# Two delta rule layers of a four-layer network: keys projected first, vector lengths taken per token, the small projections streamed over tokens, the local projections spread among the levels, and fewer idle products at the RMS norms

## The chip, the cores and the metric

One core of a Trainium2 chip runs the whole program as one launch. The metric is the device time of that launch in microseconds (us). The engines are PE (TensorE, the matrix products), DVE (VectorE), ACT (ScalarE), POOL (GpSimd) and SP (SyncE, which issues the weight loads). Each engine runs its own list of instructions strictly in order, and engines wait for one another on semaphores.

## The reference, cut to what matters

Input is 256 tokens of 1024 features. Layers 0 and 1 (softmax attention, a dense and a routed feed-forward) are not touched. Layers 2 and 3 each do this:

```python
h = rmsnorm(x, pre_mix_norm[l]); proj = h @ w_in[l]
a_qkv, a_z, a_b, a_a, b_q, b_k, b_v = split(proj)   # 3*512, 512, 4, 4, 512, 512, 512
a_qkv = silu(causal_dwconv(a_qkv, dn_conv))         # 4 taps along the tokens
aq, ak, av = l2norm(q), l2norm(k), v                # 4 heads of 128; l2norm: x * rsqrt(sum x*x + eps)
beta = sigmoid(a_b); g = -exp(a_log) * softplus(a_a + dt_bias)
o_a = gated_delta_rule(aq, ak, av, g, beta)         # needs the inverse of a unit lower triangular matrix
o_a = rmsnorm(o_a, out_norm) * silu(a_z)
o_b = dilated_attention(rope(b_q), rope(b_k), b_v)  # 8 heads of 64
x = x + rmsnorm(concat(o_a, o_b) @ w_out[l], post_mix_norm[l])
x = x + rmsnorm(conv_glu_ffn(rmsnorm(x, pre_ffn_norm[l])), post_ffn_norm[l])
```

## The kernel before, in words

Weights stream from HBM in units of 128 x 2048 float32 (1 MB) in the order that `stream_order` lists, into six buffers (`raw`). ACT rounds each unit to `w_hi` (L513) and DVE subtracts to get the rest, `w_lo` (L518). These two steps are the split. There are three buffers for split units, so the unit three places further in the stream can only be split when PE has read the present one. `walk("in", L, i)`, which stands in ACT's list and in DVE's, is that place: "unit i is read, now split the one three further on". Each projection product is done three times (hi*hi, hi*lo, lo*hi) by `mm3` (L758).

The input projection `in` has 14 units. Units 0 to 5 are query, key and value of the delta rule, two units each, done by `features` with the features on the partitions (products over 256 tokens). Numbers 3 to 6 (units 6 to 13) are the gate z, the local queries, the local keys and the local values, done by `part` in four pieces of 12 products over 512 columns (two token tiles t, two halves i of the inner dimension). Two small matrices for beta and decay, `wba`, have 8 columns.

PE's function `delta` of a layer goes in this order before the change: three projected blocks with the queries first; the 8-column products (token tiles as the stationary operand, 8 columns streamed, 48 products); projection 3; four products of ones with the squares (L1077), which give each head's length in every row, 128x512 each; projection 4; running sums of the decay (L1087, `gcol`), the decay and beta spread over rows (L1094, `grow` and `brow`); transposes of keys and values (L1102, `kn`, `vn`); the products key*key and key*query (L1112, `kk`, `kq`). Then come LEVELS = 7 levels, which invert the triangular matrix by blocks. Level 0 is a transpose (L1127); each further level is 8 products X (L1129), a copy by ACT (L1568), then 16 products D and DT (L1146), which DVE subtracts (L2196). One quarter of projection 5 stands between X and D in each of levels 1 to 4. After the levels stand eight groups of state and output products (L1157 to L1185), projection 6, the transposes of the outputs (L1194, `oT`), and then `local_attention`, which turns the rotated queries and keys (L833) and starts its scores (L804).

DVE, meanwhile: three convolution taps per block (L2084); the lengths' reciprocal (L2114) and the scaling of q and k (L2115) over 128x512 elements, four times; the decay matrix `gam` (L2127, masks added; ACT takes its exp, L1562); the blocks for the levels (L2172); after the levels the outputs, the rotation of the local queries and keys (`rope`, L1768 to L1773), and then the split of `aT_lo`, the low part of the transposed outputs (L2239).

Before the delta layer stands `enter`, the RMS norm: DVE makes a diagonal matrix from the rows' norms (`pre_scale`, L1892 and L1893), PE multiplies each token tile by it (L736), DVE applies the norm's weights (`pre_turned`, L1902, weights `prew`), ACT and DVE split the result (L1305, L1749). Between the two token tiles PE does idle products (`keep_warm`, L753), whose result nobody reads: WARM_PRE = 6 of them at the entrance of layer 2, WARM_RMS = 9 at the other three (layer 2 before the feed-forward, layer 3 twice).

## Time and profile before

| what | value |
|---|---|
| median of 3 runs | 2441.65 us (2441.45 to 2452.83) |
| profiled execution, its own time | 2445.3 us |
| its span in the trace | 2443.5 us |
| PE busy | 2290.4 us, 94% |
| DVE busy | 1745.2 us, 71% |
| ACT busy | 1382.3 us, 57% |
| mean granted TensorE clock | 0.966 of full |

PE is the engine that is nearly always busy, so a stretch gets shorter where PE has fewer or cheaper instructions, where PE waits less, or where it runs less long at the lower clock. "Busy" counts a product's whole latency; how much time a row of products takes is read from the distance of their starts.

### The profile page before, as it was taken

The page shows a single profiled execution, that of the slowest core. Times are in us where ns is not written, and L with a number is a line of the kernel's source. Part 1 is how long each engine was busy: PE and PEld are TensorE (multiplying, and loading weights), DVE is VectorE, ACT ScalarE, POOL GpSimd, SP SyncE. Part 2 cuts the span into 40 slices and gives each one's busy share as a digit, 9 for nine tenths or more (in the row PEclk, how much of TensorE's full clock was granted, in tenths as well). Part 3 has the DMA queues.
Part 4 walks back from the last instruction along what each step waited for, and adds up shares of the span by engine and source line. Part 5 has one row for each costly group of instructions (what it writes and reads, how often), then busy time and mean ns, then how long its engine had stood idle before and what let it go on. Part 6 is the DMA issues. An engine that isn't in the chain of part 4 may idle for free. (4 is left out here: it accounts for less than half of the span.)

```text
span 2443.5 us, 32636 instructions
## 1 busy us (share of the span) xinstructions
PE 2290.4 (94%) x12462; PEld 1917.8 (78%) x12462; DVE 1745.2 (71%) x1861; ACT 1382.3 (57%) x1440; POOL 55.0 (2%) x72
## 2 busy tenths in 40 slices
PE   7899999789999999999999999898799989888998
PEld 5599987568787878787878776687679978777997
DVE  5555557568888888888888898567557666765776
ACT  5433334547777777777777766352545445344544
POOL 2000000010000000000000020000000000000000
PEclk9899999899999999999999999889899999899999
DMA  9355555249999999999999998331225543122551
GB/s 390 143 194 183 183 187 173 77 153 381 355 380 359 381 356 380 358 378 359 379 359 380 358 389 324 139 138 44 95 97 183 188 157 121 69 78 96 183 188 52
DMA packets 81800, 573.37 MB, mean 235 GB/s; under 512 B 9552, under 2 KB 9664, under 8 KB 15984
## 3 DMA queue, kind: packets, MB, share of 16 engines
q1 hardware_dynamic: 76320, 545.82, 59.8%
q0 software_dynamic: 5376, 26.11, 2.9%
q8 instruction: 71, 1.16, 0.2%
q14 instruction: 33, 0.27, 0.0%
HBM read 564.03 MB, written 17.83 MB: 238 GB/s over the span
## 5 line engine op out<-in xcount | busy, mean ns | idle before, releaser
L518 DVE TENSOR_TENSOR w_lo<-raw,w_hi 128x2048 fp32r<-128x2048 f32 x508 | 1165.1, 2300 | 385.3 <-ACT w_hi L513 384.1
L513 ACT CAST w_hi<-raw 128x2048 fp32r<-128x2048 f32 x508 | 969.2, 1910 | 538.1 <-PE bank L758 532.0
L758 PE MATMUL bank<-w_hi,xT_hi 128*128 128x512 f32 x1184 | 476.1, 402 | 7.3 <-DVE w_lo L518 5.0
L758 PE MATMUL bank<-w_lo,xT_hi 128*128 128x512 f32 x1184 | 469.7, 397 | 0.0
L758 PE MATMUL bank<-w_hi,xT_lo 128*128 128x512 f32 x1184 | 468.8, 396 | 0.0
L758 PE MATMUL bank<-xT_hi,w_hi 128*128 128x256 f32 x1344 | 380.9, 283 | 11.9 <-DVE xT_lo L1749 10.0
L758 PE MATMUL bank<-xT_lo,w_hi 128*128 128x256 f32 x1344 | 380.2, 283 | 0.0
L758 PE MATMUL bank<-xT_hi,w_lo 128*128 128x256 f32 x1344 | 380.1, 283 | 0.0
L758 PE MATMUL bank<-w_hi,aT_hi 128*128 128x512 f32 x864 | 349.5, 405 | 15.1 <-DVE aT_lo L1954 9.3
L758 PE MATMUL bank<-w_lo,aT_hi 128*128 128x512 f32 x864 | 342.9, 397 | 0.0
L758 PE MATMUL bank<-w_hi,aT_lo 128*128 128x512 f32 x864 | 342.1, 396 | 0.0
L758 PEld LDWEIGHTS bank<-w_hi,xT_hi 128*128 128x128 f32 x1184 | 223.6, 189 | 67.7 <-DVE w_lo L518 9.6
L758 PEld LDWEIGHTS bank<-xT_hi,w_hi 128*128 128x128 f32 x1344 | 255.9, 190 | 14.1 <-DVE xT_lo L1749 10.6
L758 PEld LDWEIGHTS bank<-w_hi,xT_lo 128*128 128x128 f32 x1184 | 223.3, 189 | 54.8
L758 PEld LDWEIGHTS bank<-w_lo,xT_hi 128*128 128x128 f32 x1184 | 223.5, 189 | 53.6 <-issue 1.6
L758 PEld LDWEIGHTS bank<-xT_lo,w_hi 128*128 128x128 f32 x1344 | 256.1, 191 | 1.4
L758 PEld LDWEIGHTS bank<-xT_hi,w_lo 128*128 128x128 f32 x1344 | 256.0, 191 | 0.0
L758 PEld LDWEIGHTS bank<-w_hi,aT_hi 128*128 128x128 f32 x864 | 163.3, 189 | 54.4 <-issue 18.1
L758 PEld LDWEIGHTS bank<-w_hi,aT_lo 128*128 128x128 f32 x864 | 163.0, 189 | 40.0
L758 PEld LDWEIGHTS bank<-w_lo,aT_hi 128*128 128x128 f32 x864 | 163.4, 189 | 34.7
L1435 ACT ACTIVATE arena<-bank,fcw 128x256 f32<-128x256 f32 x88 | 45.0, 562 | 59.0 <-PE bank L758 59.0
L1568 ACT COPY arena<-bank 128x512 f32<-128x512 f32 x24 | 14.1, 587 | 85.7 <-PE bank L1129 85.7
(310 smaller groups left out, 1794.4 us busy)
## 6 DMA issues: line engine op xcount, KB each, us to landing
raw<-in_wu_eg SPq DMA_DIRECT2D x112, 1024.0 KB, 7.2
raw<-in_wu_eu SPq DMA_DIRECT2D x112, 1024.0 KB, 7.1
raw<-in_wu_ed SPq DMA_DIRECT2D x112, 1024.0 KB, 7.1
raw<-in_wu_up SPq DMA_DIRECT2D x44, 1024.0 KB, 4.8
raw<-in_wu_ffn_gu SPq DMA_DIRECT2D x28, 1024.0 KB, 4.8
raw<-in_wu_in SPq DMA_DIRECT2D x28, 1024.0 KB, 4.8
raw<-in_wu_down SPq DMA_DIRECT2D x22, 1024.0 KB, 4.8
raw<-in_wu_ffn_d SPq DMA_DIRECT2D x14, 1024.0 KB, 4.8
```

The lines of the kernel that those rows point to most:

```text
L513: nc.scalar.copy(w_hi[:, place(i), :], src).then_inc(*E.hi.mark("unit", i))
L518: nc.vector.tensor_tensor(w_lo[:, place(i), :], raw[:, i % RAW, :], w_hi[:, place(i), :].bitcast(F32), ALU.subtract) \
L758: mm = nc.tensor.matmul(o, l[i], r[j], start=(first and n == 0), stop=(last and n == 2), skip_group_check=not lone)
L1435: ins = nc.scalar.activation(buf[:, s % 2, m, :], bank[b + half][:, m * S:(m + 1) * S], ACT.Identity, bias=fcw[:, c, 3:4], scale=fcw[:, c, ...
L1568: nc.scalar.copy(dn["Xl"][:, t * DN_H:(t + 1) * DN_H, :], bank[t][:, :].rearrange("p (h n) -> p h n", n=P)) \
```

## The change

- **Order of the projected blocks.** The key block comes first, then query, then value. The stream's order of units is 2, 3, 0, 1, 4, ... to fit. `grow` is done after the query block, `brow` after the value block, each between projected blocks, and the transposes and key products between the halves of projection 3.
- **Lengths per token.** Instead of four products of 128x512 that put a head's length into every row, 8 products with one streamed column each give the length of (token, head) as one number (`lengths`), for keys and for queries. Keys and queries are no longer scaled themselves. The numbers go where a per-token factor stands anyway: into `gam`, `kdsc`, `bexp`, the spread beta (`brk`), and for queries into the last RMS norm (`rq`, `rq2`).
- **Small projections.** `wba` is the stationary operand (16 columns: high and low parts) and the 256 tokens are streamed; 16 products instead of 48; two small products (`fold`) bring the result back to tokens. It stands at the head of `delta`. Sigmoid is now 1/(1+exp(-x)), sharing ACT's exp.
- **Local projections among the levels.** Projections 4 and 5 both lie in levels 2 to 5, one quarter before and one after D of each level.
- **The end.** `rope` goes ahead of the outputs in DVE's list; the local queries and keys are turned before the outputs (`turn_outputs`), in other banks, and the split of `aT_lo` goes behind.
- **Entrance.** WARM_RMS is 4 and the entrance of layer 2 has no idle products. `wba`, `cw` and `prew` of both layers are loaded early (`load_both`). At layer 2, both norms are taken before the first `pre_turned`, and DVE's two splits of units stand behind.

```diff
 UNIT = 2048
-WARM_START, WARM_LN, WARM_PRE, WARM_RMS = 6, 5, 6, 9
...
                 else:
-                    yield from [(("in", L, i), "wu_in", (L - 2, i)) for i in range(14)]
...
+            def load_both():
+                gp.wait_ge(*params.last())
+                for L in (2, 3):
+                    load((wba[:, L - 2, :, :], A["wba"][L - 2], ("wba", L)), (cw[:, L - 2, :, :], A["cw"][L - 2], ("cw", L)),
+                         (prew[:, L - 2, :, :], A["prew"][L - 2], ("prew", L)))
...
-                     (fcw[:, :, :], A["fcw"][L - 2], ("fcw", L)), (prew[:, :, :], A["prew"][L - 2], ("prew", L)),
-                     (onorm[:, :], A["onorm"][L - 2], ("onorm", L)))
+                load((fcw[:, :, :], A["fcw"][L - 2], ("fcw", L)), (onorm[:, :], A["onorm"][L - 2], ("onorm", L)))
             gp.dma_start(cst[:, :], A["cst"]).then_inc(*consts.mark())
...
+                turn_heads(L, "k", lambda t, c: both(t, 4 + c), lambda t: roped.at(L, t, 0), 6)
+                turn_outputs(L)
                 turned_heads(L, 0, 0)
-                turned_heads(L, "k", 2)
...
+                def lengths(name, src, b):
+                    o = open_bank(M, b)
+                    for t in range(NT):
+                        for h in range(DN_H):
+                            c = t * DN_H + h
+                            mm = nc.tensor.matmul(o[:, c:c + 1], src[:, h, t * P:(t + 1) * P], ones[:, 0:1], start=True, stop=True)
+                    mm.then_inc(*M.groups.mark(name, L))
+
+                def project(nb, b0, units=range(2)):
+                    features([bank[b0 + j] for j in range(2)], ("in", L, 2 * nb), ("in", L, 2 * nb + 1),
+                             lambda j, m: (2 * j + m) * P, ("unit", "in", L, 2 * nb),
+                             [("cv", L, 2 * nb), ("cv", L, 2 * nb + 1)], units)
+
+                pe.wait_ge(*wsmall.at("wba"))
+                o = open_bank(M, 6)
+                for kc in range(KC):
+                    nc.tensor.matmul(o[0:16, 0:S], wba_s[:, L - 2, kc, :], xT[0][:, kc, :], start=(kc == 0), stop=False,
+                                     skip_group_check=True)
+                    mm = nc.tensor.matmul(o[0:8, 0:S], wba_s[:, L - 2, kc, 0:8], xT[1][:, kc, :], start=False, stop=(kc == KC - 1),
+                                          skip_group_check=True)
...
-                for g in range(4):
-                    pe.wait_ge(*squares.at(L, g))
-                    o = open_bank(M, 4 + g)
-                    nc.tensor.matmul(o[:, :], ones, dn["sq"][:, 4 * (g % 2):4 * (g % 2) + 4, :].rearrange("p a b -> p (a b)"),
-                                     start=True, stop=True).then_inc(*M.groups.mark("ssq", L, g))
...
+                project(1, 0, (0,))
+                pe.wait_ge(*M.free[6].at("ba", L))
+                o = open_bank(M, 7)
+                for t in range(NT):
+                    mm = nc.tensor.matmul(o[:, t * 8:t * 8 + 8], dn["baT"][:, t * P:(t + 1) * P], C("fold")[0:16, :],
+                                          start=True, stop=True)
+                mm.then_inc(*M.groups.mark("ba8", L))
+                project(1, 0, (1,))
+                for j in range(2):
+                    open_bank(M, 2 + j)
+                project(0, 2)
+                pe.wait_ge(*squares.at(L, "k"))
+                lengths("ssk", dn["sqk"], 6)
 
...
+                pe.wait_ge(*decay.at(L, "gB"))
+                for t in range(NT):
+                    heads(open_bank(M, 4 + t), "grow", t, product(lambda h: dn["gB"][:, t * DN_H + h, :], lambda h: C("upto")))
+                for j in range(2):
+                    open_bank(M, j)
+                project(2, 0)
+                pe.wait_ge(*decay.at(L, "bB"))
+                for t in range(NT):
+                    heads(open_bank(M, 2 + t), "brow", t, product(lambda h: dn["bB"][:, t * DN_H + h, :], lambda h: ident))
+                pe.wait_ge(*squares.at(L, "q"))
+                lengths("ssq", dn["sqq"], 7)
+                for t in range(NT):
+                    part("in", L, "in", 3, xT, 4, 0, t)
+                for t in range(NT):
+                    heads(open_bank(M, t), "kn", t, turn_feature(DN_H, t))
+                for t in range(NT):
+                    pe.wait_ge(*M.free[2 + t].at("brow", L, t))
+                    heads(open_bank(M, 2 + t), "kk", t, product(lambda h: dn["cv"][:, DN_H + h, t * P:(t + 1) * P],
+                                                                lambda h: dn["kb"][:, h, t * P:(t + 1) * P]))
+                for t in range(NT):
+                    part("in", L, "in", 3, xT, 4, 1, t)
+
+                pe.wait_ge(*M.act.at("silu", L, 5))
+                for t in range(NT):
+                    heads(open_bank(M, 6 + t), "vn", t, turn_feature(2 * DN_H, t))
+                for t in range(NT):
+                    heads(open_bank(M, 4 + t), "kq", t, product(lambda h: dn["cv"][:, DN_H + h, t * P:(t + 1) * P],
+                                                                lambda h: dn["cv"][:, h, t * P:(t + 1) * P]))
...
-                    if n <= 4:
-                        part("in", L, "in", 5, xT, 6, (n - 1) // 2, (n - 1) % 2)
+                    filler = {2: (4, 0), 3: (4, 1), 4: (5, 0), 5: (5, 1)}.get(n)
+                    if filler:
+                        part("in", L, "in", filler[0], xT, 6, filler[1], 0)
...
+                    if filler:
+                        part("in", L, "in", filler[0], xT, 6, filler[1], 1)
...
+            def turn_outputs(L):
                 for t in range(NT):
                     pe.wait_ge(*gated.at(L, t))
-                    o = open_bank(M, t)
+                    o = open_bank(M, 2 + t)
                     for h in range(DN_H):
                         mm = nc.tensor.transpose(o[:, h * P:(h + 1) * P], dn["o"][:, t * DN_H + h, :], ident)
                     mm.then_inc(*M.groups.mark("oT", L, t))
...
-                enter("in", WARM_PRE if L == 2 else WARM_RMS)
+                enter("in", 0 if L == 2 else WARM_RMS)
...
-                for g in range(4):
-                    ve.wait_ge(*M.free[4 + g].at("len", L, g))
-                    v = dn["cv"][:, 2 * g:2 * g + 2, :].rearrange("p a b -> p (a b)")
-                    ln = dn["sq"][:, 4 * (g % 2):4 * (g % 2) + 4, :].rearrange("p a b -> p (a b)")
-                    chain(V_.reciprocal(ln, ln))
-                    V_.scalar_tensor_tensor(v, v, (float(P) ** -0.5 if g < 2 else 1.0), ln, ALU.mult, ALU.mult) \
-                        .then_inc(*normed.mark(L, g))
-                ve.wait_ge(*normed.at(L, 3))
...
+                spread(dn["gB"], gl, "gB")
+                conv(3, 1)
+                walk("in", L, 3)
+                walk("in", L, 0)
+                conv(0, 2)
+                conv(1, 3)
+                sync()
+
+                ve.wait_ge(*M.free[6].at("ssk", L))
...
+                token_keys()
+                decayed("kk", 2, dn["AT"])
                 level_blocks(0)
-                token_keys()
-                decayed("kq", 2, dn["qk"])
+                decayed("kq", 4, dn["qk"])
+                walk("in", L, 6)
...
+                    sync()
+                    level_block(1, t)
                 token_values()
+                walk("in", L, 7)
...
-                    if n in (1, 3, 5):
-                        walk("in", L, 9 + (n - 1) // 2)
-
+                    if n >= 3:
+                        walk("in", L, 5 + n)
...
+                rope(L, (("in", 4, 6), ("in", 5, 6)), 0, 16,
+                     C("cos2").rearrange("p (a b) -> p a b", b=8), C("sin2").rearrange("p (a b) -> p a b", b=8))
...
+                ve.wait_ge(*M.act.at("oss", L))
+                V_.tensor_tensor(ss, ss, rq2, ALU.mult).then_inc(*decay.mark(L, "ss"))
                 ve.wait_ge(*M.act.at("ort", L))
                 chain(V_.reciprocal(rn8, rn8))
+                chain(V_.tensor_tensor(rn8, rn8, rq, ALU.mult))
...
-                rope(L, (("in", 4, 0), ("in", 5, 6)), 0, 16,
-                     C("cos2").rearrange("p (a b) -> p a b", b=8), C("sin2").rearrange("p (a b) -> p a b", b=8))
                 walk("in", L, 12)
...
+                if (L, which) == (2, "in"):
+                    pre_scale(L, which, rt, 1)
                 pre_turned(L, which, 0)
-                pre_scale(L, which, rt, 1)
+                if (L, which) != (2, "in"):
+                    pre_scale(L, which, rt, 1)
                 rest_T((L, which), L, 0)
                 pre_turned(L, which, 1)
                 rest_T((L, which), L, 1)
...
                     pre_scale(L, "in", "in", 0)
+                    enter(L, "in", "in")
+                    ve.wait_ge(*M.act.at("wba"))
+                    V_.tensor_tensor(wba_s[:, :, :, 8:16], wba[:, :, :, :], wba_s[:, :, :, 0:8].bitcast(F32), ALU.subtract) \
+                        .then_inc(*wsmall.mark("wba"))
                     walk("pg", 1, 2)
-                    enter(L, "in", "in")
                     walk("pg", 1, 3)
                 delta(L)
-                walk("in", L, 13)
```

Three places in the engines' lists. The first is DVE in `delta`, where lengths and decay are made (`w_lo<-raw,w_hi` is a split; the rows of the changed kernel have its own line numbers). Before:

```order
L518 TENSOR_TENSOR w_lo<-raw,w_hi 128x2048 x2
L2114 RECIPROCAL arena<-arena 128x512
L2115 SCALAR_TENSOR_TENSOR arena<-arena 128x512
...
L2115 SCALAR_TENSOR_TENSOR arena<-arena 128x512
L518 TENSOR_TENSOR w_lo<-raw,w_hi 128x2048
L2126 TENSOR_TENSOR small<-bank,small 128x4
L2127 TENSOR_TENSOR arena<-bank,msk 128x512 x2
L2132 TENSOR_TENSOR arena<-arena,bank 128x4x128 x2
```

After:

```order
L2167 RECIPROCAL small<-small 128x8
L2168 TENSOR_TENSOR small<-small 128x8
L2140 COPY arena<-small 128x1024
L2176 TENSOR_TENSOR small<-bank,small 128x4
L2177 TENSOR_TENSOR arena<-bank,msk 128x512 x2
L525 TENSOR_TENSOR w_lo<-raw,w_hi 128x2048
L2182 TENSOR_TENSOR small<-small 128x4
L2183 TENSOR_TENSOR small<-small 128x4
L2187 TENSOR_TENSOR arena<-arena,small 128x512 x2
L525 TENSOR_TENSOR w_lo<-raw,w_hi 128x2048
```

The four reciprocals over 128x512 and the four scalings (one pair of them shown) are gone; in their place stand operations on 8 numbers a row and one scaling of the decay matrix (L2187).

The second is DVE from the last level to the start of the local attention in layer 3 (`vec` holds the local queries and keys). Before:

```order
L518 TENSOR_TENSOR w_lo<-raw,w_hi 128x2048
L2196 TENSOR_TENSOR arena<-arena,bank 128x512 x2
L2207 COPY arena<-bank 128x512
...
L2219 TENSOR_TENSOR arena<-arena,bank 128x512
L2222 RECIPROCAL small<-small 128x8
L2227 SCALAR_TENSOR_TENSOR arena<-arena,small,onorm 128x128 x8
L2232 TENSOR_TENSOR arena<-arena 128x512 x2
L1768 TENSOR_TENSOR arena<-vec,cst 128x128
...
L518 TENSOR_TENSOR w_lo<-raw,w_hi 128x2048
L2239 TENSOR_TENSOR aT_lo<-bank,aT_hi 128x4x128 x2
L518 TENSOR_TENSOR w_lo<-raw,w_hi 128x2048
```

After:

```order
L2269 TENSOR_TENSOR arena<-arena,bank 128x512 x2
L525 TENSOR_TENSOR w_lo<-raw,w_hi 128x2048
L1815 TENSOR_TENSOR arena<-vec,cst 128x128
L1816 TENSOR_TENSOR arena<-vec,cst 128x128
...
L2281 COPY arena<-bank 128x512
L2284 TENSOR_TENSOR R<-arena,bank 128x512
L2288 TENSOR_SCALAR arena<-bank,small 128x128 x4
L2293 TENSOR_TENSOR arena<-arena,bank 128x512
...
L2309 TENSOR_TENSOR arena<-arena 128x512 x2
L525 TENSOR_TENSOR w_lo<-raw,w_hi 128x2048 x2
L1893 TENSOR_TENSOR aT_lo<-bank,aT_hi 128x4x128 x2
```

The rotation moved from behind the outputs to ahead of them, one more split stands ahead of it, and the subtraction for `aT_lo` stands behind both last splits.

The third is PE at the entrance of layer 2 (`R` is the diagonal matrix, `cst` the idle products). Before:

```order
L736 MATMUL bank<-R,X 128x128 x8
L753 MATMUL bank<-cst 128x512 x6
L736 MATMUL bank<-R,X 128x128 x8
L758 MATMUL bank<-xT_hi,w_hi 128x256
L758 MATMUL bank<-xT_lo,w_hi 128x256
```

After:

```order
L748 MATMUL bank<-R,X 128x128 x16
L1096 MATMUL bank<-xT_hi,wba_hi_lo 16x256
L1098 MATMUL bank<-xT_lo,wba_hi_lo 8x256
L1096 MATMUL bank<-xT_hi,wba_hi_lo 16x256
L1098 MATMUL bank<-xT_lo,wba_hi_lo 8x256
```

The idle products between the two tiles are gone, and the small projection stands first, with 256 columns streamed by each of its products.

## Rows read from the trace of the kernel before

**Rows 1.** The page, part 1: busy us (share) xinstructions.
```profile
PE 2290.4 (94%) x12462; PEld 1917.8 (78%) x12462; DVE 1745.2 (71%) x1861; ACT 1382.3 (57%) x1440; POOL 55.0 (2%) x72
```

**Rows 2.** Layer 3, PE's timeline: start, us, engine, line, operation.
```profile
2021.55 0.36 PE L758 MATMUL bank<-xT_hi,w_hi 128*128 128x256 f32 x1 [2.49 <-DVE xT_lo L1749]
...
2109.50 0.71 PE L1127 MATMUL bank<-cst,arena 128*128 128x128 f32 x5
...
2160.17 0.35 PE L1157 MATMUL bank<-R,arena 128*128 128x128 f32 x1 [0.83 <-DVE arena L2196]
...
2178.78 0.60 PE L1194 MATMUL bank<-cst,arena 128*128 128x128 f32 x4
...
2190.11 0.80 PE L804 MATMUL bank<-arena 64*128 64x128 f32 x4 [0.98 <-ACT arena L1318]
```

**Rows 3.** The same five places in layer 2.
```profile
1579.14 0.36 PE L758 MATMUL bank<-xT_hi,w_hi 128*128 128x256 f32 x1 [2.49 <-DVE xT_lo L1749]
...
1670.32 0.50 PE L1127 MATMUL bank<-cst,arena 128*128 128x128 f32 x3
...
1722.54 0.46 PE L1157 MATMUL bank<-R,arena 128*128 128x128 f32 x2 [0.83 <-DVE arena L2196]
...
1741.15 0.49 PE L1194 MATMUL bank<-cst,arena 128*128 128x128 f32 x3
...
1752.48 0.80 PE L804 MATMUL bank<-arena 64*128 64x128 f32 x4 [0.98 <-ACT arena L1318]
```

**Rows 4.** PE's waits from 1975 to 2235: us in total, times, longest.
```profile
PE bank L833 <- DVE aT_lo L2239: 5.7, 1, 5.7
PE bank L1129 <- DVE arena L2172: 5.5, 1, 5.5
```

**Rows 5.** Layer 3, PE's timeline: small projection, a filler, one level.
```profile
2055.71 0.17 PE L758 MATMUL bank<-wba_hi,xT_hi 128*128 128x8 f32 x1
...
2061.00 0.78 PE L758 MATMUL bank<-w_hi,xT_hi 128*128 128x512 f32 x1
...
2143.71 0.48 PE L758 MATMUL bank<-w_hi,xT_hi 128*128 128x512 f32 x1
...
2146.58 3.73 PE L1146 MATMUL bank<-arena 128*128 128x128 f32 x32
2150.15 1.95 PE L1129 MATMUL bank<-arena 128*128 128x128 f32 x16
```

**Rows 6.** Layer 3, DVE's timeline: taps, reciprocal, split, transposed keys.
```profile
2031.71 5.28 DVE L2084 SCALAR_TENSOR_TENSOR arena<-bank,cw,arena 128x255 f32<-128x255 f32 x12
...
2095.88 3.35 DVE L2114 RECIPROCAL arena<-arena 128x512 f32<-128x512 f32 x1
...
2099.99 2.29 DVE L518 TENSOR_TENSOR w_lo<-raw,w_hi 128x2048 fp32r<-128x2048 f32 x1
...
2109.20 2.16 DVE L2153 TENSOR_SCALAR R<-bank,small 128x128 f32<-128x128 f32 x8
```

**Rows 7.** Entrance of layer 3: timelines of PE, DVE and ACT.
```profile
2009.25 7.89 PE L753 MATMUL bank<-cst 128*128 128x512 f32 x18
...
2015.27 1.29 DVE L1902 TENSOR_TENSOR arena<-bank,prew 128x512 f32<-128x512 f32 x2 [4.60 <-DMA onorm<-in_onorm]
...
2012.15 1.88 ACT L513 CAST w_hi<-raw 128x2048 fp32r<-128x2048 f32 x1
```

**Rows 8.** Before layer 3's feed-forward: timelines of PE and DVE.
```profile
2234.78 7.89 PE L753 MATMUL bank<-cst 128*128 128x512 f32 x18
...
2239.18 0.29 DVE L1893 TENSOR_SCALAR R<-cst,small 128x128 f32<-128x128 f32 x1
```

**Rows 9.** Entrance of layer 2: PE's timeline.
```profile
1569.55 5.32 PE L753 MATMUL bank<-cst 128*128 128x512 f32 x12
```

**Rows 10.** PE's timeline, and its window: busy PE, PEld, DVE, ACT, POOL, PEclk, DMA.
```profile
1995.22 0.47 PE L758 MATMUL bank<-w_hi,aT_hi 128*128 128x512 f32 x1 [4.32 <-DVE aT_lo L1954]
...
1996.00:1999.50 3.50, 3.50 (x10) 2.73 (x9) 0.00 (x0) 0.69 (x2) 0.00 (x0) 0.52 0.43 178
```

333 lines of the change are left out of this document (166 added, 167 removed).

## The prediction

> **What bounds the kernel now.** I read the page first: PE is busy 94% of the span [rows 1], so only what PE does or waits for counts. Then I read PE's timeline over the changed stretch, from the first projected block to the first score product of the local attention. It takes 168.6 us in layer 3 [rows 2] and 173.3 us in layer 2 [rows 3], and four places cut it in pieces:
>
> - A, first block to level 0: 88.0 us in layer 3, 91.2 in layer 2.
> - B, the levels: 50.7 and 52.2.
> - C, states, outputs and projection 6: 18.6 and 18.6.
> - D, end of projection 6 to the first score: 11.3 and 11.3.
>
> PE's list of waits shows what interrupts it: 5.7 us before the turned queries for `aT_lo`, 5.5 us in level 1 for DVE's blocks [rows 4], and small ones of 1 to 3 us around the lengths and transposes. The same stand in layer 2. Last I read the granted clock: after a wait of 4.3 us TensorE is at the lower of its two levels, 1.2 instead of 2.4 GHz (0.52 of full), for the 3.5 us shown [rows 10]; PE is busy there and loses half, 1.7 us. Such stretches recur behind the waits of both layers.
>
> **Prices on PE, from distances of starts.** From 2021.55 to 2055.71 PE does six units of 48 products over 256 tokens: 0.119 us a product, 5.7 a unit [rows 2, 5]. The 48 small products take 5.3 us [rows 5]. A quarter of a projection (12 products of 512 columns) takes 2.9 us, 2143.71 to 2146.58, and 16 products of 128x128 take 3.6 us, 2146.58 to 2150.15, so four heads cost 0.9 [rows 5].
>
> **Piece A after.** The small projection is 16 products over 256 tokens, 1.9 us, and two fold products, which no row shows; bounds 0.1 and 0.5, I take 0.3. Six units: 34.3. Lengths: 16 float32 products in two groups, with one streamed column and a 128x128 stationary operand, which no row shows. The products of 128x128 are 0.22 each, which gives 3.6, and the 8-column ones 0.11 each, which gives 1.8 [rows 5]; I take the upper, being float32 too, and 0.1 a group for its end: 3.8. The running sum is 0.5. Six pairs of four-head groups (`grow`, `brow`, `kn`, `kk`, `vn`, `kq`) are 10.8. Projection 3 is 11.3. Sum 62.9 us. Projection 4, 11.3 us, has left for the levels.
>
> Does PE wait in it? I laid the three lists side by side with the durations of [rows 6]: three tap pairs of two halves 5.3 us, a split 2.3 on DVE and 1.9 on ACT. ACT's squares of the keys are ready at 21 us and PE asks for them at 25. The spread beta comes at 31, asked for at 41. The unit for projection 3 is split at 35, asked for at 45; the first block of level 0 is ready at 56, asked for at 63. The least slack is 4 us, and the four reciprocals of 3.35 us with their scalings, which stood ahead of the transposes [rows 6], are gone. So I cost the new DVE and ACT work in A at nothing; PE's own 62.9 us hide it. Were that cover gone, the price would be what each lateness adds, at most the 16 us the reciprocals and scalings had. A falls by 88.0 - 62.9 - 11.3 = 13.8 us in layer 3 and 17.1 in layer 2, net of the moved projection.
>
> **Piece B after.** PE's own: 43.7 us as before (level 0 1.8, six times X 1.8, five times D 3.6, the last D 1.8, four quarters 11.3) and 11.3 for projection 4. Levels 2 to 5 are then bound by PE, 11 us each, and DVE's 2.8 us of subtractions hide. Levels 0 and 1 stay bound by DVE: a split of 2.3 us stands right where level 0's transpose comes out, then the two halves (0.7 three times each), then the values' scaling (2.2, as the keys' in [rows 6]) and another split ahead of level 2's blocks. I get waits of 3.4 + 1.1 before level 1 and 2.5 + 0.5 before level 2. ACT empties projection 4's banks in level 4 only behind its two copies: 1.5 us. The last subtraction: 1.0. So waits are 9.9 against 7.0 before (50.7 - 43.7). B loses 2.9 us in layer 3, 1.3 in layer 2.
>
> **Piece C after.** DVE has a split and the rotation (3 us) ahead of the first output copy now, so the last output product waits some 1.5 us. C loses 1.3.
>
> **Piece D after.** The rotation is done long before. Turned queries and keys (3.6 us) and outputs (1.8) follow projection 6 at once; ACT splits one unit, then copies (2.4 us), and is done with the keys when PE is. First score 5.4 us after projection 6, not 11.3: a gain of 5.9 in each. DVE's subtraction for `aT_lo` comes just as the first scores are ready and delays them by under 0.3.
>
> So the pieces give 15.5 us in layer 3 and 20.4 in layer 2, with PE at full clock and no wait but those named. From that I take two stretches of lower clock a layer (after level 0's wait, and after the one-column products or the last output), 3.4 us, and 1.5 us a layer for small waits that I don't see: 10.6 + 15.5 = 26.1 us.
>
> **The entrances.** Layer 3 before: DVE waits 4.6 us for weights queued with `prew` [rows 7]; early loading removes it, and with four idle products (3.5 us at 7.9 for nine) the second tile starts at about 2012.8, not 2017.0. Next late is ACT, whose split of 1.9 us lies ahead of its copies until 2014.0 [rows 7]. The first block starts at about 2018.7 instead of 2021.55: 2.85 us less, but PE then stands still 4 us instead of 2.5, for which I charge one lower-clock stretch: 1.2 net. Before each feed-forward the second diagonal is ready at 2239.5 and the idle products end at 2242.6 [rows 8]: 3.0 us to gain with four idle products, less 0.8 for clock, twice: 4.4. Entrance of layer 2: six idle products stood some 5.1 us between the tiles [rows 9]. They go, and DVE's and ACT's chain behind the first tile, no longer covered, gives back 1.0: 4.1. Together 9.7.
>
> POOL issues three more small loads ahead of the experts' collection, at 0.5 us each; no engine waits for them. Two fewer activation table loads a layer lie on ACT, which has slack in A.
>
> **A rule against it.** In the trace a gap of 4.3 us was followed by half clock [rows 10]; the gap of 2.5 us at 2021.55 [rows 2] was followed by six units at 0.119 us a product throughout. So by the rows I charge 1.7 us for the entrance of layer 3 and 0.8 for each of the two before a feed-forward, 3.3 in all. By the Trainium skill, "TensorE: Matmul & The Clock Gate", section "HAM oscillation", a kernel whose PE stands still for short spells again and again falls back to the lower clock each time. By that rule each of the four entrances would pay 1.7 us more than at full clock, 6.8 us in place of 3.3, and the gain would be 3.5 us less.
>
> **Sum.** 26.1 + 9.7 = 35.8 us. The profiled execution took 2445.3 us, so 2409.5 in its terms; the median of the runs shown is 3.65 us lower, so **2406 us**.
>
> **Rivals.**
> 1. *The waits only move.* PE leaves A's waits and meets as many elsewhere, since DVE's work has shrunk but its list is still in strict order. Against it are the slacks of 4 us and more in A; for it, the 9.9 us that I see in B. Then what remains is the smaller projection (3.1 us a layer), the freed `aT_lo` wait (5.9 a layer) less C and B (2.9 + 1.3 and 1.3 + 1.3), and half of the entrances: 18 - 6.8 + 4.8 = 16 us, 2426.
> 2. *No lower clock.* A denser PE stays at full clock throughout: 15.5 + 20.4 + 2.85 + 3.0 + 3.0 + 4.1 = 48.9 us, 2393. For it, gaps are shorter; against it, no stretch of these two layers before was free of it.
> 3. *Splits starve PE: slower.* In the new lists a split stands behind a tap or a wait for a small operation. If it came late for each unit, PE would stand still for a split's 1.9 + 2.3 = 4.2 us at up to 28 units, 118 us, and the time would be 2441.65 - 35.8 + 118, about 2523 us. It ends slower than before from 1.3 us a unit on average (35.8 / 28), and slower by the 12 us that a measurement tells from 1.7. Against it, I count 7 to 14 us of slack for each unit in A.
>
> **How the numbers follow.** Forecast, 2393 to 2424: 0.82. Rival 1 beyond that: 0.10, of which 0.05 still faster. Rival 2 below 2393: 0.03. Rival 3: 0.04 slower; 0.01 for slower in another way. 0.5% is 12.2 us, about what a measurement of this kernel can tell from no change. Faster is then 0.90, same 0.05, slower 0.05. The unknown prices (lengths 1.8 to 3.6 us, fold 0.1 to 0.5, clock 0 to four stretches a layer, entrances 4.8 to 13.0) span 2393 to 2418 by themselves; with half of rival 1 the range is 2393 to 2424.
>
> **What would show it.** The stretch from first projected block to first score falls to about 158 us in both layers; A to about 64 and D to about 5.5; B rises to 62 to 65 with its waits in levels 1 and 2. The wait before the turned queries is gone. DVE has no reciprocal of 128x512 outside layers 0 and 1. The rest of the program is unchanged. I am wrong if PE waits for splits inside A, if the one-column products cost far more than 0.24 us each, or if lower-clock stretches follow every entrance.

## The result, and the profile after

The changed kernel takes 2371.49 us (median of 4 runs, 2370.11 to 2372.58) against 2443.89 us in the same measurement: a ratio of 0.9706, 95% interval 0.9682 to 0.9729. The forecast was 2406 with a range of 2393 to 2424. The direction was right and the gain twice as large, 72 us in place of 36.

The page's first part after, to be set against [rows 1]:

```profile
PE 2233.2 (94%) x12412; PEld 1907.0 (80%) x12412; DVE 1717.1 (72%) x1876; ACT 1371.4 (58%) x1423; POOL 54.3 (2%) x72
```

PE is still busy 94% of the span. The five places of [rows 2] in layer 3, now with the small projection as the first:

```profile
1963.80 0.28 PE L1096 MATMUL bank<-xT_hi,wba_hi_lo 128*16 128x256 f32 x1 [4.09 <-DVE xT_lo L1796]
...
2026.30 0.38 PE L1162 MATMUL bank<-cst,arena 128*128 128x128 f32 x2
...
2090.41 0.79 PE L1195 MATMUL bank<-R,arena 128*128 128x128 f32 x5 [0.83 <-DVE arena L2269]
...
2109.56 0.71 PE L843 MATMUL bank<-cst,vec 128*128 128x128 f32 x5
...
2114.45 0.80 PE L814 MATMUL bank<-arena 64*128 64x128 f32 x4 [2.11 <-ACT arena L1358]
```

And the same in layer 2, against [rows 3]. The third row in each is the end of the levels, the fourth the end of projection 6, the last the first score product.

```profile
1548.20 0.37 PE L1096 MATMUL bank<-xT_hi,wba_hi_lo 128*16 128x256 f32 x1 [2.75 <-DVE wba_hi_lo L2460]
...
1612.07 1.04 PE L1162 MATMUL bank<-cst,arena 128*128 128x128 f32 x8
...
1675.97 0.79 PE L1195 MATMUL bank<-R,arena 128*128 128x128 f32 x5 [0.83 <-DVE arena L2269]
...
1695.13 1.04 PE L843 MATMUL bank<-cst,vec 128*128 128x128 f32 x8
...
1700.02 1.33 PE L814 MATMUL bank<-arena 64*128 64x128 f32 x13 [2.11 <-ACT arena L1358]
```

| piece | layer 3 before, forecast, after | layer 2 before, forecast, after |
|---|---|---|
| A, first block to level 0 | 88.0, 62.9, 62.5 | 91.2, 62.9, 63.9 |
| B, levels | 50.7, 64.9, 64.1 | 52.2, 64.9, 63.9 |
| C, to the end of projection 6 | 18.6, 19.9, 19.2 | 18.6, 19.9, 19.2 |
| D, to the first score | 11.3, 5.4, 4.9 | 11.3, 5.4, 4.9 |
| sum | 168.6, 153.1 (+ 4.9), 150.7 | 173.3, 153.1 (+ 4.9), 151.8 |

(Forecast: by the terms in its text; the 4.9 us of lower clock and small waits were charged to the stretch as a whole.) So this part came out near the terms, 2.4 and 1.3 us under their sum, and without the 4.9. PE's list of waits in the whole of layers 2 and 3, us in total, times, longest:

```profile
PE bank L1164 <- DVE arena L2234: 9.1, 3, 4.2
PE bank L748 <- DVE R L1946: 8.8, 4, 4.1
PE bank L770 <- DVE aT_lo L2007: 6.7, 2, 4.4
PE bank L823 <- DVE arena L1858: 6.2, 2, 3.4
```

The first is the wait before level 1: 4.2 us in layer 2, 4.2 and 0.7 in layer 3, forecast 3.4 and 1.1. The wait for `aT_lo` before the turned queries [rows 4] is gone. The waits forecast before level 2 (2.5 and 0.5 us) did not come: 0.3 us in layer 2, none in layer 3. Instead level 1 ran at the lower clock. The products X of levels 1, 2 and 3 in layer 2 (L1164; the gap before each in brackets):

```profile
1617.33 4.00 PE L1164 MATMUL bank<-arena 128*128 128x128 f32 x16 [4.22 <-DVE arena L2234]
...
1626.02 2.33 PE L1164 MATMUL bank<-arena 128*128 128x128 f32 x16 [0.33 <-issue]
...
1637.25 1.95 PE L1164 MATMUL bank<-arena 128*128 128x128 f32 x16
```

The window of the first of them (length, then busy us of PE, PEld, DVE, ACT and POOL, granted clock, DMA share, GB/s) has a granted clock of 0.50:

```profile
1617.30:1621.00 3.70, 3.67 (x16) 3.53 (x17) 3.67 (x11) 0.58 (x1) 0.00 (x0) 0.50 0.57 241
```

**Where the 72 us lie.** I cut both traces at the first diagonal product of each entrance and at the first projected product behind it. The differences of the stretches' lengths, changed kernel less kernel before:

| stretch | us |
|---|---|
| all ahead of layer 2's entrance (1566.05 to 1539.13) | -26.9 |
| the four entrances together (55.2 to 43.2) | -12.0 |
| layer 2, delta rule to output projection (217.9 to 196.0) | -21.9 |
| layer 3, the same (211.4 to 195.9) | -15.5 |
| dense layer of 2 (196.4 to 196.8) | +0.4 |
| dense layer of 3, to the end (196.6 to 199.8) | +3.3 |
| sum (spans 2443.5 and 2370.8) | -72.7 |

The first row is what the forecast denied: "The rest of the program is unchanged." Nothing that PE, DVE or ACT does in layers 0 and 1 or in the experts is touched (POOL issues some small loads earlier), yet 27 us are gone there. The transposes inside the experts show it. The view of their line gives shortest, median and longest in ns, then the start of the first and of the last. Before, 945.8 us apart:

```profile
L1024 PE MATMUL bank<-cst,arena x224: 270/272/273, 558.4 to 1504.2; 128*128 128x128 f32 x112
```

After, 925.0 us apart:

```profile
L1035 PE MATMUL bank<-cst,arena x224: 270/272/273, 552.8 to 1477.8; 128*128 128x128 f32 x112
```

What got faster are the products of 512 columns. The page's groups before: busy us, mean ns of one.

```profile
L758 PE MATMUL bank<-w_lo,xT_hi 128*128 128x512 f32 x1184 | 469.7, 397 | 0.0
L758 PE MATMUL bank<-xT_lo,w_hi 128*128 128x256 f32 x1344 | 380.2, 283 | 0.0
```

After:

```profile
L770 PE MATMUL bank<-w_lo,xT_hi 128*128 128x512 f32 x1184 | 460.9, 389 | 0.0
L770 PE MATMUL bank<-xT_lo,w_hi 128*128 128x256 f32 x1344 | 382.9, 285 | 0.0
```

The means hold each product's latency. The pitch is in the distance of starts. In the dense layer of layer 2, 24 products of 512 columns from `aT` and then 96 of 256 columns alternate; before:

```profile
1869.23 0.39 PE L758 MATMUL bank<-w_hi,aT_hi 128*128 128x512 f32 x1
...
1874.83 0.28 PE L758 MATMUL bank<-xT_hi,w_hi 128*128 128x256 f32 x1
...
1886.18 0.39 PE L758 MATMUL bank<-w_hi,aT_hi 128*128 128x512 f32 x1
```

and after:

```profile
1830.94 0.40 PE L770 MATMUL bank<-w_hi,aT_hi 128*128 128x512 f32 x1
...
1836.41 0.28 PE L770 MATMUL bank<-xT_hi,w_hi 128*128 128x256 f32 x1
...
1847.92 0.40 PE L770 MATMUL bank<-w_hi,aT_hi 128*128 128x512 f32 x1
```

5.60 against 5.47 us for the 24, 11.35 against 11.51 for the 96: the one kind got 2% faster, the other 1% slower. (The expectations below give such runs from first start to last end, 0.16 us more.)

The suspect is in the change, but in no instruction: `fold` adds 8 columns to `cst`, and all tensors allocated behind it move 32 bytes on in every partition's SBUF. From the program's allocations, `w_hi` starts at byte 65664 in both kernels; `xT_hi` at 134752 before and 134784 after; `xT_lo`, `aT_hi` and `aT_lo` follow it at multiples of 8192.

### The profile page after: what moved, and what is told of

Read it like the earlier page. It is cut to its first block and busy times, and to the rows that moved or that the text cites. A ratio compares the mean times of both kernels' runs of the same rounds, so it can differ in the third digit from the quotient of the medians.

```text
span 2370.8 us, 32516 instructions
## 1 busy us (share of the span) xinstructions
PE 2233.2 (94%) x12412; PEld 1907.0 (80%) x12412; DVE 1717.1 (72%) x1876; ACT 1371.4 (58%) x1423; POOL 54.3 (2%) x72
## 5 line engine op out<-in xcount | busy, mean ns | idle before, releaser
L770 PE MATMUL bank<-w_hi,xT_hi 128*128 128x512 f32 x1184 | 468.2, 395 | 10.7 <-DVE w_lo L525 5.9
L770 PE MATMUL bank<-w_hi,xT_lo 128*128 128x512 f32 x1184 | 461.4, 390 | 0.0
L770 PE MATMUL bank<-w_lo,xT_hi 128*128 128x512 f32 x1184 | 460.9, 389 | 0.0
L770 PEld LDWEIGHTS bank<-w_hi,xT_hi 128*128 128x128 f32 x1184 | 222.3, 188 | 63.9 <-DVE w_lo L525 11.6
L770 PEld LDWEIGHTS bank<-xT_hi,w_hi 128*128 128x128 f32 x1344 | 260.8, 194 | 8.8 <-DVE xT_lo L1796 5.3
L1615 ACT COPY arena<-bank 128x512 f32<-128x512 f32 x24 | 14.1, 586 | 91.9 <-PE bank L1164 91.9
```

Of the source, the lines that this page charges most:

```text
L770: mm = nc.tensor.matmul(o, l[i], r[j], start=(first and n == 0), stop=(last and n == 2), skip_group_check=not lone)
L1615: nc.scalar.copy(dn["Xl"][:, t * DN_H:(t + 1) * DN_H, :], bank[t][:, :].rearrange("p (h n) -> p h n", n=P)) \
```

## Experiments

### Is it the place in SBUF, and of what?

Eight unused columns at the end of the constants, in the kernel before (e1) and in the changed one (e2):

```diff
     parts["rms_eps"] = np.full((P, 1), RMS_EPS)
+    parts["unused"] = np.zeros((P, 8))
```

e3, the kernel before with `xT` and `aT` alone moved; e4 has a third pad of 8 columns ahead of `X`, which puts `X` and `R`, and the masks, `vec`, `small` and the arena behind `aT`, at multiples of 64 bytes, and `xT` and `aT` 32 beyond one. The two pads that both have:

```diff
+        pad1 = sb("pad1", [P, 8])
         xT = [sb(f"xT_{part}", [P, KC, S], F32R) for part in ("hi", "lo")]
         aT = [sb(f"aT_{part}", [P, KC, S], F32R) for part in ("hi", "lo")]
+        pad2 = sb("pad2", [P, 8])
```

e1: 

> The kernel before with eight unused columns at the end of the constants, and nothing else: every tensor that is allocated behind the constants (X, R, the turned tokens xT and aT, the masks, vec, small, the arena) starts 32 bytes later, at a multiple of 64 bytes where it started 32 beyond one. This is what the changed kernel does by the way, with its eight columns of fold. Theory T1 (the place of the tensors in SBUF sets the speed of the 128x512 products, whose stationary operand is xT or aT; it is the missed half of the gain): the turn of the eight experts goes from 122.4 us to about 119.7, the mean of the 512-column products from 397 to about 389 ns, the layers 0 and 1 end 5 us earlier, and the whole is 27 to 33 us faster, near 2412. Rival T2 (the faster products come of something else in the change: other loads, other order, the chip of the day): no change, within 3 us of the kernel before.

e2: 

> The changed kernel with eight unused columns more at the end of the constants, so that the tensors behind them start 32 bytes beyond a multiple of 64 again, as in the kernel before. T1: the turn of the experts goes back to 122.4 us, and the time to 2398 to 2408, which is near the forecast of 2406. T2: 2371, as the changed kernel.

e3: 

> The kernel before with eight unused columns ahead of xT and eight behind aT: xT and aT alone start at a multiple of 64 bytes; X, R, the masks, vec, small and the arena start 32 beyond one, as before. T1 with the operands of TensorE as the cause (xT and aT are the stationary operand of the 512-column products): all of the gain of the first run of this call, 27 to 33 us. If instead X, R, vec or the arena (operands of VectorE, ScalarE and DMA) are the cause: no change, 2442. T2: no change.

e4: 

> The complement: the kernel before with X, R, the masks, vec, small and the arena at a multiple of 64 bytes, and xT and aT 32 bytes beyond one. T1 with the operands of TensorE as the cause: the expert turn stays at 122.4 us and the time within 5 us of the kernel before. If the other operands are the cause: 27 to 33 us faster. T2: no change.

Measured, with 2441.14 us for the kernel before: e1 2418.22 (ratio 0.9897, interval 0.9879 to 0.9916), e2 2389.72 (0.9783, 0.9768 to 0.9799), e3 2419.38 (0.9907, 0.9891 to 0.9923), e4 2440.45 (0.9995, 0.9981 to 1.0008). The transposes inside the experts in e3, 925.5 us from first to last:

```profile
L1026 PE MATMUL bank<-cst,arena x224: 270/272/273, 552.9 to 1478.4; 128*128 128x128 f32 x112
```

and in e4, 946.0 us:

```profile
L1027 PE MATMUL bank<-cst,arena x224: 270/272/273, 555.3 to 1501.3; 128*128 128x128 f32 x112
```

The start of `xT` and `aT` is the cause, and nothing else that moved with it. Unused columns alone make the kernel before 25 us faster by the ratio (23 by the medians), and make the changed one 19 us slower by the ratio (18 by the medians). Cut like the table above, e1's trace has 1541.0 us ahead of layer 2's entrance, 25 less than the kernel before, which is nearly all of that table's first row. The pitches give the same: 5040 products of 512 columns stand there, each 5.4 ns cheaper, and 1344 of 256 columns, each 1.6 ns dearer, 27 - 2 = 25 us (an estimate from the starts above).

e2 does not bring the old distance back, though. From `w_hi` to `xT_hi`, modulo 256 bytes, it is 224 in the kernel before, 0 in e1, e3 and the changed kernel, and 32 in e2 and e4. What the change does otherwise has to be read at one distance. At 0 it is the changed kernel against e1, 0.9706 against 0.9897 or 2371.49 against 2418.22 us: 47 us. At 32 it is e2 against e4, 2389.72 against 2440.45: 51 us. e4 also shows that a cheaper product need not reach the end: 96 products of 256 columns take 11.36 us in it and 11.52 in the kernel before, about 6.7 us over all 4032 of them by this estimate, and the whole is 0.7 us shorter.

### Which rule sets the speed?

e5 puts `xT` 64 bytes off, e6 the weights 32 bytes off, e10 all tensors 32 off:

```diff
+    parts["unused"] = np.zeros((P, 16))
```

That is e5. e6 and e10 have these pads, and e10 has 8 unused columns as well:

```diff
+        pad1 = sb("pad1", [P, 8])
         w_hi = sb("w_hi", [P, SPLIT, UNIT], F32R)
         w_lo = sb("w_lo", [P, SPLIT, UNIT], F32R)
+        pad2 = sb("pad2", [P, 24])
         cst = sb("cst", [P, NC])
```

e5: 

> The changed kernel with sixteen unused columns at the end of the constants: xT, aT and all behind them start at a multiple of 64 bytes still, but 64 beyond a multiple of 128 (in the changed kernel at a multiple of 128). If 64 bytes are the unit that counts: 2371, as the changed kernel, with 5.63 us for 24 products of 512 columns from aT. If it is 128 bytes: those go back to 5.76 us, and the time towards 2390.

e6: 

> The changed kernel with w_hi and w_lo 32 bytes later, xT, aT and all else at the same place modulo 128 bytes. The 512-column products have w as the moving operand and xT or aT as the stationary one, the 256-column products the other way round. If the start of the stationary operand decides (64-byte multiples are fast): the 512-column products stay at 389 to 392 ns (5.63 us for 24), and the 256-column ones, whose stationary operand is now off, get slower, by up to 5 ns each of 4032, some 20 us: near 2390. If the start of the moving operand decides: the 512-column products change and the 256-column ones stay at 285 ns (11.67 us for 96). If only the distance of the two operands decides: both change, the 512-column ones back to 397 ns (about 2385 to 2395).

e10: 

> The changed kernel with w_hi and w_lo, and also xT, aT and the rest, 32 bytes beyond a multiple of 128. So far 24 products of 512 columns took 5.63 us only where both operands start at a multiple of 128, and 5.75 to 5.78 us where xT and aT lie 32, 64 or 96 bytes off and where w lies 32 off. If what counts is that the two operands lie alike modulo 128 bytes: 5.63 us again here, and with 11.36 us for 96 products of 256 columns about 2358. If each has to start at a multiple of 128: 5.77 us, and 2388 to 2408.

e5 took 2390.13 us (0.9793, 0.978 to 0.9807), so 64 bytes is not the unit. e6 took 2407.97 (0.9866, 0.9851 to 0.9881): moving the weights slows the 512-column products as much as moving the tokens. e10 took 2393.28 (0.9796, 0.9776 to 0.9816), which seemed to speak for starts at multiples of 128. But the two operands of e10 stand 128 bytes apart modulo 256, so three rules for fast 512-column products were left. A: each operand starts at a multiple of 128 bytes. B: the two are alike modulo 256. C: both start at 128 modulo 256. The next three runs told them apart; the pads are 32 columns ahead of `X` (f1), 8 ahead of `w_hi` (f2) and 32 ahead of `w_hi` (f3).

f1: 

> The changed kernel with 32 unused columns ahead of X: X, xT, aT and all behind them 128 bytes on, at a multiple of 128 bytes still, but 128 apart from w modulo 256. Rule A (each operand at a multiple of 128 bytes): 5.63 us for 24 products from aT, 2371. Rule B (both operands alike modulo 256) and rule C (both at 128 modulo 256): 5.74 to 5.78 us, 2388 to 2395.

f2: 

> The changed kernel with 8 unused columns ahead of w_hi: w_hi, w_lo and all behind them 32 bytes on, all distances as in the changed kernel. Rule B (relative): 5.63 us for 24 products from aT and 11.67 for 96 products of 256 columns, 2371. Rules A and C (absolute): 5.74 to 5.78 us, 2388 to 2400.

f3: 

> The changed kernel with 32 unused columns ahead of w_hi: all from w_hi on 128 bytes on, all distances as in the changed kernel, w, xT and aT at multiples of 256. Rules A and B: 5.63 us for 24, 2371. Rule C (both at 128 modulo 256): 5.74 to 5.78 us, 2388 to 2400.

f1 took 2398.04 us (0.9819, 0.9792 to 0.9847), f2 2371.61 (0.9708, 0.968 to 0.9736), f3 2372.41 (0.9715, 0.9686 to 0.9744). The experts' transposes in f1, 943.8 us apart:

```profile
L1036 PE MATMUL bank<-cst,arena x224: 269/272/273, 558.5 to 1502.3; 128*128 128x128 f32 x112
```

and in f2, 925.3 us apart, where every operand is 32 bytes off a multiple of 128:

```profile
L1036 PE MATMUL bank<-cst,arena x224: 269/272/273, 552.3 to 1477.6; 128*128 128x128 f32 x112
```

Of the three rules only B fits: the 512-column products are fast when the two operands are alike modulo 256 bytes, wherever they stand (f2, f3). The runs by that distance (from the weights to `xT` and `aT`), first start to last end of a run of products in the two dense layers:

| distance mod 256 | runs | 24 of 512 columns, us | 96 of 256 columns, us |
|---|---|---|---|
| 0 | after, e1, e3, f2, f3 | 5.63 | 11.68 |
| 32 | e2, e4 | 5.76 | 11.36 to 11.37 |
| 64 | e5 | 5.76 to 5.77 | 11.46 to 11.47 |
| 96 | e6 | 5.77 to 5.79 | 11.67 to 11.68 |
| 128 | e10 | 5.73 to 5.76 | 11.68 in layer 2, 11.55 in layer 3 |
| 128 | f1 | 5.73 to 5.74 | 11.55 to 11.56 |
| 224 | before | 5.76 | 11.52 to 11.53 |

The 512-column products, whose moving operand is the weights, are fast at distance 0 alone (160 and 192 were not tried); the 256-column ones, whose moving operand is the tokens, like 32 best and are near their worst at 0. Modulo 256 and not 512: in e9 and f4 `aT` stands 256 on modulo 512 and its 24 products take 5.63. At 128 the last column has two values, even within e10, so that distance is not all that sets the pitch of the 256-column products, and what else does is open.

### Both speeds in one kernel

If so, the tokens can stand at distance 0 where 512-column products prevail (layers 0, 1, experts) and at 32 where 256-column ones do. e9 gives layers 2 and 3 a second view of the same memory:

```diff
+        xT_mem = [sb(f"xT_{part}", [P, KC * S + 32], F32R) for part in ("hi", "lo")]
+        xT, xT_on = [[a[:, at:at + KC * S].rearrange("p (c n) -> p c n", n=S) for a in xT_mem] for at in (0, 8)]
```

> The changed kernel, in which layers 2 and 3 keep their turned tokens 32 bytes further on in the same memory (xT_on), while layers 0 and 1 and the experts keep xT at a multiple of 128 bytes. By the pitches of the runs so far: the 4032 products of 256 columns run at 11.36 in place of 11.67 us for 96, 13.0 us less; the 384 products of 512 columns from xT in these layers go from 5.63 to 5.76 us for 24, 2.1 us more; so 10.9 us faster than the changed kernel, 2360 to 2362. Rival: it is not the start of xT that set the 256-column products but another tensor that moved with it: 2371 or more.

It took 2373.37 us (0.972, 0.97 to 0.9739), a miss. In this kernel tile 0 of layer 2 is written over columns of tile 1 that layer 1's gate still reads, so it computes with wrong tokens there, and its time alone is used. Layer 2's entrance began at 1549.09, 10 us later than in the changed kernel, since the pad had put `xT_lo` 128 bytes away from `w_hi` modulo 256, which the rule of that moment (multiples of 128) called harmless; its dense layers were 2.3 and 3.5 us shorter. f4 mends both: one tensor for the two parts, and the second view only from layer 2's dense layer on.

```diff
+        xT_mem = sb("xT", [P, 2 * KC * S + 64], F32R)
+        xT, xT_on = [[xT_mem[:, at + i * KC * S:at + (i + 1) * KC * S].rearrange("p (c n) -> p c n", n=S) for i in range(2)]
+                     for at in (0, 8)]
+        def turned_at(L, which=None):
+            return xT_on if L == 3 or (L == 2 and which in ("mix", "gu")) else xT
```

> The changed kernel with xT_hi and xT_lo in one tensor at their places of before and, from layer 2's dense layer on, a second view 32 bytes further on (layers 0, 1, the experts and layer 2's delta rule keep the first; in the earlier run with two views tile 0 of layer 2 was written over columns of tile 1 that layer 1's gate still read, and xT_lo stood 128 bytes further on). The 256-column products of both dense layers and of layer 3 at 11.36 to 11.47 us for 96 in place of 11.67; in the pieces of the runs so far the two dense layers are 4.3 us (all 32 off) to 6 us (two views) shorter, layer 3 the same. So 2365 to 2368, if nothing else moves. Rival: 2371, the chain on VectorE and the weights' arrival take up what the products give.

2365.36 us (2363.91 to 2366.01; ratio 0.9684, 0.9661 to 0.9707), against 2371.61 and 2372.41 for f2 and f3, which run as the changed kernel does, on the same chip. The 24 and the 96 products in its dense layer:

```profile
1847.01 0.39 PE L775 MATMUL bank<-w_hi,aT_hi 128*128 128x512 f32 x1
...
1852.47 0.40 PE L775 MATMUL bank<-xT,w_hi 128*128 128x256 f32 x2
...
1863.68 0.39 PE L775 MATMUL bank<-w_hi,aT_hi 128*128 128x512 f32 x1
```

5.46 and 11.21 us: each kind at its best. This is the fastest of all kernels here.

### What are the fewer idle products worth?

```diff
-WARM_START, WARM_LN, WARM_RMS = 6, 5, 4
+WARM_START, WARM_LN, WARM_RMS, WARM_PRE = 6, 5, 9, 6
...
-                enter("in", 0 if L == 2 else WARM_RMS)
+                enter("in", WARM_PRE if L == 2 else WARM_RMS)
```

That is e7. e11 sets WARM_RMS to 0 in the changed kernel; e12 sets WARM_RMS to 4 and WARM_PRE to 0 in the kernel before.

e7: 

> The changed kernel with the idle products as before: 9 in place of 4 at RMS (layer 3's entrance and both entrances of the dense layers), 6 in place of none at layer 2's entrance. Theory T3 (the entrances gain what the forecast gave them, since the clock loses nothing): 9.7 us slower by the forecast, 12.4 by the pieces of the two traces, so 2381 to 2384. Rival: the idle products had kept the clock up, and the delta layers and dense layers run longer at the lower clock without them: 2371 to 2374.

e11: 

> The changed kernel without any idle products at RMS (0 in place of 4). The 8 that are left take 3.60 us ahead of each dense layer and 4.6 in layer 3's entrance, and a wait of 1.31 us for VectorE follows; without them at most 2.3 us of each can be saved, 6 to 7 us in all, if the clock stays as it is: 2365. From the run with the idle products restored (12.7 us more in the entrances, 3.5 more in the whole): three quarters are given back at the lower clock, so 2369 to 2373.

e12: 

> The kernel before with the changed kernel's numbers of idle products alone (4 in place of 9 at RMS, none in place of 6 at layer 2's entrance). By the forecast's terms for the entrances 9.7 us faster, 2431 to 2432. By the run with the idle products restored in the changed kernel: 2 to 5 us faster, since the stretches behind the entrances lose the clock, 2436 to 2439.

e7: 2374.97 us (0.9725, 0.9712 to 0.9738), 3.5 us slower than the changed kernel, a difference that is small against the two intervals. e12: 2436.86 (0.998, 0.9968 to 0.9992), 4.3 us faster than the kernel before, between 2 and 8 by its interval. Both point to some 4 us, not 9.7. They don't ask quite the same, though: e12's entrances are only 7.8 us shorter (55.2 to 47.4), since layer 3's, which still waits for the weights queued with `prew`, is 1.7 us longer. e11: 2374.02 (0.9723, 0.9703 to 0.9743), no faster than with four; its entrances before the dense layers take 13.0 us in place of 11.2 and 11.3, for the second tile's diagonal products then run at half clock. The windows behind the entrances show where the rest goes. First the changed kernel (layer 2's dense layer, layer 3, its dense layer):

```profile
1755.40:1952.20 196.80, 190.35 (x1321) 178.69 (x1321) 136.62 (x163) 95.78 (x103) 0.00 (x0) 0.98 0.50 177
1964.00:2159.70 195.70, 179.24 (x1168) 159.32 (x1167) 118.75 (x228) 92.93 (x166) 1.59 (x3) 0.93 0.27 95
2171.00:2370.50 199.50, 190.18 (x1320) 178.57 (x1320) 134.68 (x163) 91.18 (x99) 0.00 (x0) 0.97 0.40 143
```

Then e7:

```profile
1760.70:1956.00 195.30, 188.84 (x1320) 177.27 (x1321) 136.63 (x163) 95.79 (x103) 0.00 (x0) 0.99 0.50 178
1970.10:2163.20 193.10, 176.88 (x1168) 157.67 (x1169) 118.81 (x228) 92.90 (x166) 1.58 (x3) 0.94 0.27 96
2177.20:2373.50 196.30, 187.25 (x1320) 176.03 (x1320) 134.74 (x163) 91.21 (x99) 0.00 (x0) 0.99 0.40 145
```

With the same instructions each stretch is 1.5 to 3.2 us shorter at a clock 0.01 to 0.02 higher. The entrances of e7 are 12.7 us longer together (9.1, 11.2, 11.6 and 11.3 us become 13.9, 14.0, 14.1 and 13.9), its four stretches behind them (layer 2's too, 196.0 to 193.2) 10 us shorter. The first 10 us of layer 2's dense layer in the changed kernel and in e7, at a granted clock of 0.83 and 1.00:

```profile
1755.40:1765.40 10.00, 9.99 (x71) 10.00 (x72) 4.59 (x3) 2.60 (x2) 0.00 (x0) 0.83 0.55 210
1760.70:1770.70 10.00, 9.98 (x83) 10.00 (x84) 6.07 (x3) 3.63 (x4) 0.00 (x0) 1.00 0.55 211
```

Layer 3's dense layer has the same two values. The delta layers begin at 0.83 to 0.85 in both kernels; what they lose lies further on.

### The small projection

e8 keeps its new place at the head of the layer but takes the old form, 48 products with the tokens as the stationary operand, straight into bank 7; ACT's copy and the fold are gone.

```diff
-                for kc in range(KC):
-                    nc.tensor.matmul(o[0:16, 0:S], wba_s[:, L - 2, kc, :], xT[0][:, kc, :], start=(kc == 0), stop=False,
-                                     skip_group_check=True)
...
+                for t in range(NT):
+                    for kc in range(KC):
+                        mm = mm3(o[:, t * 8:t * 8 + 8], [a[:, kc, t * P:(t + 1) * P] for a in xT],
+                                 [wba_s[:, L - 2, kc, 0:8], wba_s[:, L - 2, kc, 8:16]], kc == 0, kc == KC - 1)
```

> The changed kernel with the small projection in its old form (48 products whose stationary operand is the tokens, 8 columns each, straight into the bank that the decay reads), at the new place, ahead of the keys. By the forecast's terms (5.3 us old, 1.9 and 0.3 new) 3.1 us slower per layer: 2378. By the changed kernel's trace, where the streamed form took 3.3 us and its fold 0.6 in layer 2 at the lower clock, between 1.4 us faster and 3 us slower per layer: 2369 to 2377. Rival: no change, since the levels' chain on VectorE is what ends last: 2371.

A miss: 2387.37 us (0.9779, 0.9766 to 0.9793), 16 us slower than the changed kernel; its profiled execution was a faster one than its median, with a span only 8.8 us longer. The 48 products in layers 2 and 3 of e8, at a granted clock of 0.50 from start to end:

```profile
1547.80:1558.20 10.40, 10.15 (x48) 10.18 (x48) 4.40 (x2) 0.00 (x0) 0.00 (x0) 0.50 0.54 203
1967.50:1978.00 10.50, 10.23 (x48) 10.26 (x49) 2.01 (x1) 0.00 (x0) 0.00 (x0) 0.50 0.28 100
```

The streamed form in the changed kernel, for the most part at the lower of the two levels:

```profile
1548.20:1551.40 3.20, 3.20 (x16) 2.09 (x17) 3.20 (x2) 0.00 (x0) 0.00 (x0) 0.53 0.12 20
1963.80:1967.00 3.20, 3.20 (x17) 2.19 (x18) 1.84 (x1) 0.00 (x0) 0.00 (x0) 0.56 0.20 28
```

10.4 against 3.2 us and 0.6 for the fold: 6.6 us a layer, not the forecast's 3.1. I had priced the old form at the 5.3 us of its old place [rows 5], where PE ran at full clock in layer 3; behind the entrance's wait the old form runs at 0.50 and the new one at 0.53 and 0.56. In this trace the two delta stretches are 12.1 us longer, near the 13 of two layers of 6.6, and the dense layers 3.3 us shorter. Why the median moved by 16 us I can't say.

## Why the prediction was wrong

- **The step that failed** is "The rest of the program is unchanged", and with it the sum, which had no term for where tensors stand. Of the 72 us, 23 to 25 come from the 32 bytes (e1). With the operands alike in both kernels the change is worth 47 us (distance 0) or 51 (distance 32), where the forecast had 36; from the 2441.65 us that it started from, that is 2395, inside its range, or 2391, 2 us under it. No row that I read of before could have shown it, but the change could: it widens a tensor ahead of the operands of nearly every product.
- **Pieces A to D** were right to 1.0 us each (first table). For the levels (B) that is in part luck: the 3.0 us of waits before level 2 did not come, and about as much was lost to the lower clock in level 1 (X 4.00 us and D 4.57 in layer 2, at full clock 1.95 and 3.73). The forecast's 20.4 us for layer 2 is 20.2 by its own cuts (173.3 - 153.1).
- **The lower clock in the delta layers** is the second term that failed: "two stretches of lower clock a layer ... 3.4 us, and 1.5 us a layer for small waits that I don't see" took 9.8 us off the gain. The stretch gained 17.9 and 21.5 us, more than the undiminished 15.5 and 20.4. The lower clock did come, in level 1 and in the small projection (3.2 us, forecast 1.9), but the waits that the terms held and that did not come paid for it. It is not the placement: e1's trace has 426.7 us in the two delta stretches (first product behind the entrance to the next entrance), the changed kernel's 391.9, 34.8 less, where the forecast gave 26.1. The granted clock of layer 2, first projected product to output projection, rose. Rival 2, no lower clock, comes closest with its gain of 48.9 us, against 47 and 51 at like places; its condition was not met, so the number is luck. The window of layer 2 before, granted clock 0.89:

```profile
1579.10:1797.00 217.90, 191.98 (x1172) 167.77 (x1173) 132.21 (x221) 98.11 (x174) 2.17 (x4) 0.89 0.25 88
```

and in the changed kernel, 0.92; in layer 3 it stayed at 0.93.

```profile
1548.20:1744.20 196.00, 179.53 (x1169) 159.54 (x1170) 121.12 (x229) 93.05 (x166) 2.17 (x4) 0.92 0.28 103
```

- **The lengths** cost 1.84 us a group of 8, 3.7 us a layer (forecast 3.8); that they were worth their change on DVE was argued from the forecast's reciprocals and not tried by itself.
- **The entrances** were wrong in the other way: they shortened by 12.0 us (forecast 9.7), but only about 4 us of such a cut reach the end (e7, e12). The forecast charged 3.3 us for the clock in them; what is lost lies behind them, 10 us in four stretches of 200 us (e7). The rule of the Trainium skill weighed there ("TensorE: Matmul & The Clock Gate", section "HAM oscillation") pointed the right way: the first 10 us behind each of the four entrances run at 0.83 to 0.85. The loss was larger than it was given.
- **Rival 1** (waits only move) and **rival 3** (splits starve PE) did not come: the gain was larger than forecast, and no wait for a split unit (`w_lo`) is in PE's list for these layers.
- **The small projection's form** was worth twice its term, for the clock at its new place (e8).

## What to carry to other kernels

Compare a stretch that the change doesn't touch first; if it moved, print where the operands stand before looking for a cause in the schedule. A tensor that gets wider moves all behind it, and unused columns are a cheap control for any change that adds a tensor. Price a moved instruction at the clock of its new place, and judge idle products by the whole time, not by the gap they fill.

## What the runs showed of the hardware

- For these float32r products, the distance between the starts of the stationary and the moving operand in SBUF, modulo 256 bytes, changes the pitch. 24 products of 128x512 take 5.63 us at distance 0 and 5.73 to 5.79 us at 32, 64, 96, 128 and 224; 96 products of 128x256 with the operands' roles exchanged take 11.36 us at 32 and 11.68 at 0. At distance 0, moving both operands together by 32 or 128 bytes changes nothing (f2, f3). At 128 the 256-column products have two values, 11.55 and 11.68, within one kernel (e10). The mechanism behind all this is open.
- 48 products with 8 streamed columns took 5.3 us at full clock [rows 5] and 10.4 us at 0.50 (e8), nearly twice.
- Idle products between two tiles shortened what came behind them: with 9 in place of 4, the first 10 us of the dense layer ran at a granted clock of 1.00 in place of 0.83 (e7).
